# A hybrid S5 and GLA layer on one core: the GLA passes moved ahead of the S5 scan, scan temporaries in PSUM

## The chip, the cores and the metric

The kernel runs on one core of a Trainium2 chip. The metric is the time of one execution in microseconds (us). The five engines of the core work from queues of their own: PE is TensorE (matrix products; PEld are its weight loads), DVE is VectorE, ACT is ScalarE, POOL is GpSimd, and SP only issues DMAs here. They meet through semaphores alone.

## The reference

One layer over 512 latent tokens (`lat`) and 256 context tokens (`ctx`) of width 1024, in fp32: a half-step SwiGLU (ffn1), a token mixer, a second half-step SwiGLU (ffn2), a last norm. Each is preceded by an RMS norm with shift and scale and followed by a gate; these nine vectors come from a linear map of the conditioning (`ada_w`, nine groups of 1024 columns). The mixer, cut to what matters:

```python
u, q, k, v, r, glr, ga, gb = split(h @ w_in)            # 512,256,256,512,512,32,1024,1024
ya = s5_branch(u)      # per group of 16 channels: h_t = lam * h_(t-1) + B u_t (complex, 64 states),
                       # both directions; y = gelu(Re(C h) + d u); ya = y * sigmoid(y @ glu_w + b)
yb = gla_branch(q, k, v, glr)   # chunks of 64 tokens, 4 heads, both directions:
                       # log decay = logsigmoid(glr @ gate_up + b) / 16, cumulated in the chunk,
                       # masked scores q k^T inside, a carried state k^T v across chunks
yb = rms_norm(yb) * silu(r)
y = (sigmoid(ga) * (ya @ s5_out) + sigmoid(gb) * (yb @ gla_out)) @ w_o
```

## The kernel before

**Products.** Each fp32 product is made of three matmuls: every weight block and every moving block is split in a high and a low part, and `split_mm` (L795) adds lo*hi, hi*lo and hi*hi. Weights come in units of 512 KB. SP loads them into four slots of `w_raw`; POOL makes `w_hi` (L724) and `w_lo` (L727) of each, 3.5 us in all, once the last job that used the slot four units before is done (`last_user`). The order of units is written out in the table UNIT.

**Jobs.** TensorE's work is numbered in the table JOB. Job j writes PSUM slot j % 4: `lat(j)` is its even bank, `ctx_(j)` its odd bank (eight banks of 512 fp32). TensorE may start job j when slot_read says that job j - 4 was read; it adds to job_done at its end. A job of a projection with 128 output channels is 24 matmuls of 512 columns (`tall_jobs`, L1013), with 24 more of 256 if the context is wanted (k, v, glr). u is made of 8 jobs (`wide_jobs`, L996), each for every eighth token and with all four slots of weights.

**Order of TensorE in the mixer.** u (8 jobs, the first waits for one row of h after another while `norm` makes them), glr, k, ada7, q, ada8, the chunks (transposes `ut` of u, the four r, `xs`: state inputs of the scan), v (4), its transposes vt (6), ga (8), gb (8), z0 (gate logits), y (8 jobs: S5 outputs from ut, the scanned states xs and hb, with three matrices per group streamed from HBM into `stream2`), yt, z1, glu (4). Then four GLA passes p (two head pairs x two directions): ket (transposes of the decayed keys), sc (scores, two jobs), kv (two jobs), and after every second pass out (4 jobs). Eight products of `ya @ s5_out`, called ma, are spread between them (`MA_AFTER`). Then ybt (transposes of the GLA output), mb (8 products of `yb @ gla_out`), wo (8), the norm and ffn2.

**The S5 scan** runs on DVE alone (`advance`, L1961 on, called 21 times): five tensor_tensor instructions a step, a product with the real part of a power of lambda (L1980), two halves with the imaginary part (L1981, L1982), two additions to `xs` (L1984, L1986). Powers (`lam_p`) and temporaries (`st1`, `st2`) lie in SBUF. Its steps: three over the context (16, 8 and 4 blocks of 64 elements), 7 of 512 elements, 7 of 64, 4 of 896. It begins when ACT has read the last xs job and must end before y (states_ok).

**GLA chain of one pass.** ACT's `softplus(p)` reads z (three activations, table loads between), DVE's `cumulate(p)` makes the cumulated decays (L2027 to L2036), ACT's `decays(p)` the exponentials, DVE's `decayed(p)` the scaled q and k (L2043 to L2052), then ket and sc on TensorE, ACT copies ket, DVE masks the scores (L2095) and after kv carries the states (L2118, L2120; s_ok). Its buffers lie where h was, so nothing of it could start before gb was done.

**ada groups.** DVE adds up each of the late groups from eight tiles of 512 KB in a ring of two (`ada_add`); group 7 and 8 are loaded at the mixer's start, and TensorE sums each in ada_job.

The head of the chunks' order and the place of the products ma:

```python
CHUNK_ORDER = [("ut", 4), ("r", 1), ("ut", 4), ("r", 1), ("xs", 6), ("r", 1), ("xs", 6), ("r", 1), ("xs", 4)]
MA_AFTER = {("kv", 0): 2, ("kv", 1): 2, ("kv", 2): 1, ("kv", 3): 2, ("out", 3): 1}
```

## Time and profile before

| | |
|---|---|
| median of 3 runs | 1567.67 us (1566.15 to 1569.5) |
| profiled execution, its own time | 1567.58 us |
| its span | 1565.6 us |
| mean granted clock of TensorE | 0.966 |
| busy: PE, PEld, DVE, ACT, POOL | 93%, 81%, 48%, 17%, 43% |
| mixer, first matmul of u to first of wo | 683.7 to 1127.5 us |

A busy TensorE may still run at half its clock (1.2 instead of 2.4 GHz); the column PEclk of a stretch gives the mean granted clock, 1.00 being 2.4 GHz. Idle time is told with the engine or DMA whose semaphore ended it.

### The profile page before, as it was taken

How to read it: one execution, taken by the hardware profiler on the slowest of the kernel's cores; microseconds unless marked ns; L12 is line 12 of the kernel's file. 1: busy time of each engine (PE TensorE's matmuls, PEld its weight loads, DVE VectorE, ACT ScalarE, POOL GpSimd, SP SyncE). 2: the span in 40 equal slices, each digit the busy share in tenths (PEclk: the TensorE clock that was granted, in tenths of full speed). 3: DMA queues.
4: the chain of work that ended last, by engine and by line, in shares of the span. 5: the costliest groups of instructions: out<-in, count | busy, mean ns of one | idle time of the engine just before them, and what ended most of it. 6: DMA issues, size and time to landing. Idle time of an engine off the chain costs nothing.

```text
span 1565.6 us, 18786 instructions
## 1 busy us (share of the span) xinstructions
PE 1461.8 (93%) x7780; PEld 1261.9 (81%) x7780; DVE 757.3 (48%) x1004; ACT 268.5 (17%) x418; POOL 675.9 (43%) x389
## 2 busy tenths in 40 slices
...
GB/s 295 93 186 61 111 148 111 105 148 103 123 150 74 132 153 41 56 93 99 174 154 102 122 128 159 156 16 23 139 135 67 82 107 95 94 95 93 105 72 54
DMA packets 232561, 174.28 MB, mean 111 GB/s; under 512 B 28664, under 2 KB 212124, under 8 KB 232476
## 3 DMA queue, kind: packets, MB, share of 16 engines
...
q8 instruction: 61, 1.00, 0.3%
...
HBM read 155.26 MB, written 17.79 MB: 111 GB/s over the span
## 4 chain that ended last, share of the span: by engine, by line
PE 85%; DVE 8%; ACT 2%; issue 2%; SPq 1%; DMA 0%; DVEq 0%; POOL 0%; ACTq 0%; PEldq 0%; POOLq 0%
PE ps L795 58%; PE ps L966 14%; PE ps L969 4%; PE ps L826 2%; PE ps L804 2%; DVE ssq L1763 1%; PE ps L888 1%; PE ps L879 1%; PE ps L1055 1%; DVE h_lo L1799 1%; SPq L663 1%; PE ps L1204 1%; PE ps L1208 1%; DVE gu L1785 0%; DVE y L2068 0%
## 5 line engine op out<-in xcount | busy, mean ns | idle before, releaser
L724 POOL TENSOR_SCALAR w_hi<-w_raw 128x1024 fp32r<-128x1024 f32 (+2 forms) x187 | 214.0, 1145 | 825.2 <-issue 464.2
L727 POOL TENSOR_TENSOR w_lo<-w_raw,w_hi 128x1024 fp32r<-128x1024 f32 (+2 forms) x187 | 460.2, 2461 | 15.6
L795 PE MATMUL ps<-h_hi,w_lo 128*128 128x384 f32 (+2 forms) x1344 | 419.8, 361 | 13.1 <-DVE h_lo L1799 5.6
L795 PE MATMUL ps<-h_lo,w_hi 128*128 128x384 f32 (+2 forms) x1344 | 415.0, 358 | 0.0
L795 PE MATMUL ps<-h_hi,w_hi 128*128 128x384 f32 (+2 forms) x1344 | 414.9, 358 | 0.0
L795 PEld LDWEIGHTS ps<-h_hi,w_lo 128*128 128x128 f32 (+1 forms) x1344 | 241.4, 188 | 45.1 <-issue 7.1
L795 PEld LDWEIGHTS ps<-h_hi,w_hi 128*128 128x128 f32 (+1 forms) x1344 | 244.0, 188 | 24.2
L795 PEld LDWEIGHTS ps<-h_lo,w_hi 128*128 128x128 f32 (+1 forms) x1344 | 244.0, 188 | 23.4
L1840 DVE SCALAR_TENSOR_TENSOR ps<-ps,silu 128x768 f32<-128x768 f32 (+1 forms) x44 | 36.6, 832 | 283.5 <-PE ps L795 283.5
L1864 DVE SCALAR_TENSOR_TENSOR x<-ps,mod,x 128x512 f32<-128x512 f32 x96 | 70.7, 748 | 171.5 <-PE ps L969 94.0
L966 PE MATMUL ps<-act_hi,w_lo 128*128 128x512 f32 x352 | 140.2, 398 | 1.8 <-DVEq L1845 1.8
L966 PE MATMUL ps<-act_lo,w_hi 128*128 128x512 f32 x352 | 138.4, 393 | 0.0
L966 PE MATMUL ps<-act_hi,w_hi 128*128 128x512 f32 x352 | 138.3, 393 | 0.0
L1384 ACT ACTIVATE silu<-ps 128x768 f32<-128x768 f32 (+1 forms) x44 | 31.1, 707 | 514.4 <-PE ps L795 514.3
L1742 DVE SCALAR_TENSOR_TENSOR ada_acc<-ada_w,cs,ada_acc 128x1024 f32<-128x1024 f32 x70 | 100.7, 1471 | 21.7 <-DMA ada_w<-in_ada_w_dram 20.4
L1397 ACT ACTIVATE act_hi<-ps 128x768 fp32r<-128x768 f32 (+1 forms) x44 | 31.1, 707 | 316.0 <-DVE ps L1840 316.0
L966 PEld LDWEIGHTS ps<-act_hi,w_lo 128*128 128x128 f32 x352 | 66.6, 189 | 20.2 <-DVEq L1845 4.7
L966 PEld LDWEIGHTS ps<-act_hi,w_hi 128*128 128x128 f32 x352 | 66.4, 189 | 14.7
L966 PEld LDWEIGHTS ps<-act_lo,w_hi 128*128 128x128 f32 x352 | 66.4, 189 | 14.5
L1843 DVE TENSOR_TENSOR act_lo<-ps,act_hi 128x768 fp32r<-128x768 f32 (+1 forms) x44 | 36.3, 825 | 37.4 <-ACT act_hi L1397 37.4
L969 PE MATMUL ps<-act_hi,w_lo 128*128 128x256 f32 x176 | 49.4, 280 | 0.0
L969 PE MATMUL ps<-act_hi,w_hi 128*128 128x256 f32 x176 | 49.3, 280 | 0.0
...
## 6 DMA issues: line engine op xcount, KB each, us to landing
...
```

The lines of the kernel that those rows point to most:

```text
L724: pool.tensor_scalar(w_hi[:, s, 0:cols], w_raw[:, s, 0:cols], 1.0, 1.0, ALU.mult, ALU.mult)\
L727: pool.tensor_tensor(w_lo[:, s, 0:cols], w_raw[:, s, 0:cols], w_hi[:, s, 0:cols].bitcast(F32), ALU.subtract).then_inc(w_split, 1)
L795: last = pe.matmul(mv[2], st, mv[part], start=(first and q == 0), stop=(n == len(terms) - 1 and q == 2))
L804: return pe.transpose(o, i, ident[0:i.shape[0], 0:i.shape[0]])
L826: last = pe.matmul(o, cs[:, k, :], first_tile(g, k)[:, 512 * q:512 * q + 512], start=(k == 0), stop=(k == KD - 1))
L966: last = pe.matmul(lat(j), st[:, k, c], mv[:, k, 0:NL], start=(k == 0 and r == 0), stop=(k == tiles - 1 and r == 2))
L969: last = pe.matmul(ctx_(j)[:, 0:NC], st[:, k, c], mv[:, k, NL:NT], start=(k == 0 and r == 0), stop=(k == tiles - 1 and r == 2))
L1384: act.activation(dst, src, ACT.Silu).then_inc(slot_read[jg % 4], 1)
L1742: STT(acc, tile, cs[:, k, v:v + 1], acc, ALU.mult, ALU.add).then_inc(acc_ok, 1)
L1840: STT(up, up, 0.5, sl, ALU.mult, ALU.mult).then_inc(gu_ok, 1)
L1843: TT(lo, up, hi.bitcast(F32), ALU.subtract).then_inc(act_lo_ok, 1)
L1864: ins = STT(x[:, k, 0:NL], lat(j), mod[:, g, 0:1], x[:, k, 0:NL], ALU.mult, ALU.add)
```

## The change

The mixer's work is put in another order, and buffers are laid out anew for it; the products and their number stay the same.

- TensorE starts with k0, k1 and q0 together, one k-step of all three for each row of h; then glr, q1, z0, z1, ada7, v and vt. The GLA passes follow (`GLA_ORDER`), with four of the gb products (gbA) and the eight u jobs between their steps in place of ma; then the chunks with ybt among them, gbB (4), ga (8), y, yt, mbA (4), glu (4), mbB (4), ma (8), wo.
- The scan's powers lie in the odd PSUM banks 1 and 3 and its temporaries in banks 5 and 7. A bank holds 512 elements, so the step of 1024 becomes two of 512 and the four of 896 become eight of 448: 26 calls. The powers are made in SBUF (`lam_s`) and copied.
- Scores use 64 of the 128 rows (kz, qz without zero halves), in one job over both banks of a slot.
- The GLA product is kept in SBUF times its gate (`mb`), and the S5 product is made last and added to it. sigmoid and product of the GLU are written back to PSUM.
- SP: the S5 output matrices of the first three batches are loaded earlier, gates later; v3's weights stand between tiles 1 and 2 of ada group 7. Group 8 is loaded in ffn2's first segment, a tile behind each weight unit, added by DVE there, summed by TensorE behind the last up product of that segment.

```diff
+_number(UNIT, [("ffn1", FFN_UNITS), ("k", 2), ("q0", 1), ("glr", 1), ("q1", 1), ("v", 4), ("gbA", 4), ("u", 4), ("r", 4),
+               ("gbB", 4), ("ga", 8), ("mbA", 2), ("glu", 2), ("mbB", 2), ("ma", 4), ("wo", 8), ("ffn2", FFN_UNITS)])
+GLA_ORDER = [("ket", 0, 1), ("sc", 0, 1), ("kv", 0, 2), ("gbA", 0, 1), ("gbA", 1, 1), ("z", 2, 1),
+             ("ket", 1, 1), ("sc", 1, 1), ("kv", 1, 2), ("gbA", 2, 1), ("out", 1, 4), ("gbA", 3, 1), ("z", 3, 1),
+             ("ket", 2, 1), ("sc", 2, 1), ("kv", 2, 2), ("u", 0, 1), ("u", 1, 1), ("u", 2, 1),
+             ("ket", 3, 1), ("sc", 3, 1), ("kv", 3, 2), ("u", 3, 1), ("u", 4, 1), ("u", 5, 1), ("u", 6, 1),
+             ("out", 3, 4), ("u", 7, 1)]
-CHUNK_ORDER = [("ut", 4), ("r", 1), ("ut", 4), ("r", 1), ("xs", 6), ("r", 1), ("xs", 6), ("r", 1), ("xs", 4)]
+CHUNK_ORDER = [("ut", 4), ("r", 1), ("ut", 4), ("r", 1), ("xs", 6), ("r", 1), ("xs", 6), ("r", 1), ("ybt", 4), ("xs", 4)]
...
+    def lam_p(c):
+        return ps[:, 2 * c + 1, :].rearrange("p (k g) -> p k g", g=DG)
+    def scan_part(c, shape):
+        return ps[:, 5 + 2 * c, 0:int(np.prod(shape))].rearrange("p (k g) -> p k g", g=DG)
...
@@ SP
+                        if not with_ada and part.segs + i == 0:
+                            ada_tile(ADA_MIX + 1, v)
...
+            for k in range(KD):
+                ada_tile(ADA_MIX, k)
+                if k == 1:
+                    tall(UNIT["v"] + 3, 1, C_V + 3 * P)
+            tall(UNIT["gbA"], 4, C_GB)
+            wide(UNIT["u"], C_U)
+            tall(UNIT["r"], 4, C_R)
...
+            for b in range(3):
+                y_matrices(b)
+            tall(UNIT["ga"] + 4, 4, C_GA + 4 * P)
+            half_units("mbA", out_b, 0)
+            half_units("glu", glu_w, 0)
+            is_done(sp, JOB["ga"] + 7)
...
+            for t in range(4):
+                load_gate(KD + t)
+            for b in range(3, 8):
+                y_matrices(b)
@@ TensorE
+            first = [("k", 0, JOB["k"], NT), ("k", 1, JOB["k"] + 1, NT), ("q0", 0, JOB["q0"], NL)]
...
+            for k in range(KD):
+                pe.wait_ge(h_ok, KD + k + 1)
+                for i in range(len(first)):
...
+            tall_job("glr", 0, JOB["glr"], NT, 2 * RANK)
+            tall_job("q1", 0, JOB["q1"], NL)
+            gate_logits(0)
+            gate_logits(1)
+            ada_job(ADA_MIX, JOB["ada7"])
+            for q in range(4):
+                tall_job("v", q, JOB["v"] + q, NT)
...
+            for t in range(6):
+                was_read(pe, JOB["vt"] + t)
...
+                for t in range(4):
+                    for hp in range(2):
+                        r = slice(64 * hp, 64 * hp + 64)
+                        last = pe.matmul((lat, ctx_)[hp](j)[:, P * t:P * t + P], kz[r, P * t:P * t + P],
+                                         e1q[r, P * t:P * t + P], start=True, stop=True)
@@ ACT
+            softplus(0)
+            softplus(1)
+            evac_tokens(JOB["v"], v_t[:, 0, :], NT, P)
+            decays(0)
+            for q in range(1, 4):
+                evac_tokens(JOB["v"] + q, v_t[:, q, :], NT, P)
+            decays(1)
+            for t in range(6):
+                take_v(t)
+            take_keys(0)
+            for q in range(2):
+                take_gate(GJ["gbA", q], KD + q)
+            softplus(2)
+            take_keys(1)
+            decays(2)
+            take_gate(GJ["gbA", 2], KD + 2)
+            take_out(1)
+            take_gate(GJ["gbA", 3], KD + 3)
+            softplus(3)
+            take_keys(2)
+            decays(3)
...
@@ DVE
+            for p in range(4):
+                masked(p)
+                states(p)
+                if p < 3:
+                    decayed(p + 1)
+                if p < 2:
+                    cumulate(p + 2)
...
-                TT(t1, prev, c_re, ALU.mult).then_inc(scan_step, 1)
-                TT(part(t2, low), part(prev, high), part(c_im, high), ALU.mult).then_inc(scan_step, 1)
-                TT(part(t2, high), part(prev, low), part(c_im, low), ALU.mult).then_inc(scan_step, 1)
+                TT(part(0, every), prev, c_re, ALU.mult).then_inc(scan_step, 1)
+                TT(part(1, slice(*low)), rows(prev, high), rows(c_im, high), ALU.mult).then_inc(scan_step, 1)
+                TT(part(1, slice(*high)), rows(prev, low), rows(c_im, low), ALU.mult).then_inc(scan_step, 1)
                 dve.wait_ge(scan_step, n0 + 1)
-                TT(cur, cur, t1, ALU.add).then_inc(scan_step, 1)
+                TT(cur, cur, part(0, every), ALU.add).then_inc(scan_step, 1)
                 dve.wait_ge(scan_step, n0 + 4)
-                TT(cur, cur, t2, ALU.add).then_inc(scan_step, 1)
+                TT(cur, cur, part(1, every), ALU.add).then_inc(scan_step, 1)
...
+            def ya_low(c):
+                j = JOB["glu"] + c
+                dve.wait_ge(yah_ok, c + 1)
+                TT(ya_lo[:, c, :], lat(j), ya_hi[:, c, :].bitcast(F32), ALU.subtract).then_inc(slot_read[j % 4], 1)
```

## Rows read from the trace of the kernel before

**Rows 1.** Page part 1: busy time of TensorE, share of the span, instructions.
```profile
PE 1461.8 (93%) x7780; PEld 1261.9 (81%) x7780; DVE 757.3 (48%) x1004; ACT 268.5 (17%) x418; POOL 675.9 (43%) x389
```

**Rows 2.** Page part 4: the chain that ended last, shares of the span by engine.
```profile
PE 85%; DVE 8%; ACT 2%; issue 2%; SPq 1%; DMA 0%; DVEq 0%; POOL 0%; ACTq 0%; PEldq 0%; POOLq 0%
```

**Rows 3.** Five stretches: length; busy us (x instructions) of PE, PEld, DVE, ACT, POOL; clock; DMA share; GB/s.
```profile
683.70:740.90 57.20, 53.15 (x192) 45.84 (x192) 24.01 (x34) 10.89 (x20) 1.99 (x6) 0.84 0.34 111
825.00:950.60 125.60, 123.97 (x600) 103.98 (x600) 120.84 (x120) 19.23 (x32) 73.01 (x37) 1.00 0.40 108
950.60:981.30 30.70, 24.30 (x197) 21.99 (x196) 13.85 (x17) 16.84 (x22) 1.79 (x2) 1.00 0.78 220
981.30:1005.00 23.70, 16.54 (x84) 12.87 (x85) 18.60 (x12) 15.62 (x17) 17.40 (x9) 0.78 0.19 61
1005.00:1095.00 90.00, 70.09 (x577) 56.43 (x575) 61.34 (x95) 30.55 (x49) 14.55 (x8) 0.89 0.17 54
```

**Rows 4.** List of waits of TensorE: who waited for whom, total us, times, longest.
```profile
PE ps L804 <- DVE ke L2047: 8.8, 2, 4.7
PE ps L795 <- DVE y_lo L2063: 6.3, 1, 6.3
PE ps L804 <- DVE o_sb L2135: 5.8, 1, 5.8
PE ps L804 <- ACT v_t L1442: 1.6, 1, 1.6
PE ps L795 <- POOL w_lo L727: 1.4, 1, 1.4
```

**Rows 5.** Timeline of PE, first projection: start, us, instruction, [idle before <- releaser].
```profile
697.36 0.76 PE L795 MATMUL ps<-w_hi,h_lo 128*96 128x512 f32 x1 [0.93 <-DVE h_lo L1799]
...
702.13 0.40 PE L795 MATMUL ps<-w_hi,h_hi 128*96 128x512 f32 x1
702.37 0.40 PE L795 MATMUL ps<-w_hi,h_lo 128*96 128x512 f32 x1
```

**Rows 6.** Timeline of DVE: adds of ada group 7.
```profile
711.14 1.28 DVE L1742 SCALAR_TENSOR_TENSOR ada_acc<-ada_w,cs,ada_acc 128x1024 f32<-128x1024 f32 x1 [2.05 <-DMA ada_w<-in_ada_w_dram]
714.09 1.29 DVE L1742 SCALAR_TENSOR_TENSOR ada_acc<-ada_w,cs,ada_acc 128x1024 f32<-128x1024 f32 x1 [1.66 <-DMA ada_w<-in_ada_w_dram]
```

**Rows 7.** Timelines of DVE and ACT: one softplus, cumulate and decays; take_v.
```profile
861.51 3.05 ACT L1474 ACTIVATE v_sb<-ps 128x512 f32<-128x512 f32 x6 [0.98 <-PE ps L804]
...
957.65 1.02 DVE L2027 TENSOR_SCALAR g_b<-ps,vt 128x768 f32<-128x768 f32 x1 [1.93 <-ACT g_a L1492]
...
963.19 0.63 ACT L1499 ACTIVATE g_a<-g_b 128x512 f32<-128x512 f32 x1 [1.99 <-DVE g_d L2036]
...
965.88 0.69 DVE L2043 TENSOR_TENSOR e1q<-qt,g_a 128x512 f32<-128x512 f32 x1 [2.72 <-ACT g_c L1503]
```

**Rows 8.** Timeline of DVE: the S5 scan and the copy to hb.
```profile
825.44 2.04 DVE L1980 TENSOR_TENSOR st<-xs,lam_p 128x1024 f32<-128x1024 f32 x1 [36.30 <-ACT xs L1467]
...
865.51 0.69 DVE L1980 TENSOR_TENSOR st<-xs,lam_p 128x512 f32<-128x512 f32 x1
...
869.12 0.69 DVE L1980 TENSOR_TENSOR st<-xs,lam_p 128x512 f32<-128x512 f32 x1
...
876.31 2.77 DVE L1980 TENSOR_TENSOR st<-xs,lam_p 128x512 f32<-128x512 f32 x1
...
895.46 0.22 DVE L1980 TENSOR_TENSOR st<-xs,lam_p 128x64 f32<-128x64 f32 x1
...
950.79 1.23 DVE L2013 COPY hb<-xs 128x2048 f32<-128x2048 f32 x1 [0.66 <-PE ps L795]
```

**Rows 9.** Groups of DVE by form: x count | busy, mean ns | idle before.
```profile
L1864 DVE SCALAR_TENSOR_TENSOR x<-ps,mod,x 128x512 f32<-128x512 f32 x96 | 70.7, 748 | 171.5 <-PE ps L969 94.0 <-PE ps L966 77.5
...
L1763 DVE TENSOR_TENSOR ssq<-ssq,silu 128x512 f32<-128x512 f32 x14 | 14.6, 1042 | 0.3
```

More of the change, by code:

```diff
@@ new lines @@
+_number(JOB, [("vec", 1), ("x", KD), ("skip", 2), ("xh", 14), ("row1", 1), ("row0", 1), ("col1", 1), ("col0", 1), ("lam", 1),
+              ("ffn1", FFN1_JOBS), ("norm1", 2), ("k", 2), ("q0", 1), ("glr", 1), ("q1", 1), ("z0", 1), ("z1", 1),
+              ("ada7", 1), ("v", 4), ("vt", 6), ("gla", GLA_JOBS), ("chunks", 32), ("gbB", 4), ("ga", 8), ("y", 8),
+              ("yt", 4), ("mbA", 4), ("glu", 4), ("mbB", 4), ("ma", KD), ("wo", KD), ("norm2", 2), ("ffn2", FFN2_JOBS),
+              ("norm3", 1), ("out", 4)])
@@ L163 @@
 NADA = 9 * KD
 GJ = {("z", 0): JOB["z0"], ("z", 1): JOB["z1"]}
[L169 to L170 removed]
 def _gla_jobs():
     n = JOB["gla"]
[L175 to L183 removed]
+    for name, p, count in GLA_ORDER:
+        GJ[(name, p)] = n
+        n += count
@@ L950, in seg @@
                             last = ada_sums(ada_cols(j, ADA_COL), g)
+                        if not two and nth == 0 and v == 2 * tiles - 1:
+                            pe.wait_ge(acc_ok, ada_added(ADA_MIX + 1, KD))
+                            last = ada_sums(ada_late(j), ADA_MIX + 1)
                         last.then_inc(job_done, 1)
@@ new lines, in _, with gate_logits @@
+            tall_job("glr", 0, JOB["glr"], NT, 2 * RANK)
+            tall_job("q1", 0, JOB["q1"], NL)
+            def gate_logits(p):
+                ti, d = p // 2, p % 2
+                j = GJ["z", p]
+                wait_read(pe, j)
+                for q in range(2):
+                    last = pe.matmul((lat, ctx_)[q](j)[:, 0:384], gate_up[:, d, P * ti:P * ti + P],
+                                     glr[:, 384 * q:384 * q + 384], start=True, stop=True)
+                last.then_inc(job_done, 1)
@@ new lines, in _ @@
+            for name, p, _ in GLA_ORDER:
+                if name == "ket":
+                    turn_keys(p)
+                elif name == "sc":
+                    scores(p)
+                elif name == "kv":
+                    key_values(p)
+                elif name == "out":
+                    readout(p)
+                elif name == "z":
+                    gate_logits(p)
+                elif name == "gbA":
+                    tall_job("gbA", p, GJ["gbA", p], NL)
+                else:
+                    wide_job("u", GJ["u", p], lambda h, k: h[:, k, p:NT:CH], NCH)
@@ L1060, in state_inputs, with turn_o @@
                     pe.sem_inc(st_used, 1)
+            def turn_o(c, j):
+                pe.wait_ge(ybtok_ok, 1)
+                wait_read(pe, j)
+                for t in range(4):
+                    last = transpose(lat(j)[:, P * t:P * t + P], o_sb[:, t, P * c:P * c + P])
+                last.then_inc(job_done, 1)
             for name, b, j in CHUNK_JOBS:
@@ L1215, in _ @@
[L1215 to L1223 removed]
+            for i in range(4):
+                out_product("mbA", i, JOB["mbA"] + i, yb_hi, yb_lo, None if i else yb_ok)
@@ L1224, in _ @@
+            for i in range(4):
+                out_product("glu", i, JOB["glu"] + i, y_hi, y_lo, None if i else yl_ok)
+            for i in range(4):
+                out_product("mbB", i, JOB["mbB"] + i, yb_hi, yb_lo)
+            for c in range(4):
+                was_read(pe, JOB["glu"] + c)
+            for i in range(KD):
+                out_product("ma", i, JOB["ma"] + i, ya_hi, ya_lo)
             for q in range(KD):
@@ L1509, in _ @@
+            for q in range(4):
+                take_gate(JOB["gbB"] + q, KD + 4 + q)
+            for q in range(8):
+                take_gate(JOB["ga"] + q, q)
+            for c in range(4):
+                was_read(act, CJ["ybt", c])
+                act.activation(yb_hi[:, c, :], r_sb[:, c, :], ACT.Copy).then_inc(ybh_ok, 1)
             for b in range(8):
                 j = JOB["y"] + b
-                if b == 2:
-                    decays(0)
                 is_done(act, j)
```

888 lines of the change are left out of this document (411 added, 477 removed).

## The prediction

> **What bounds the kernel now.** I read the page first, then the chain, then stretches, then single waits. TensorE is busy 93% of the span [rows 1], and 85% of the chain that ended last runs over it, with DVE next at 8% [rows 2]. So only two things pay: time in which TensorE stands or runs at the lower clock, and work that leaves it. The change alters no product of the projections, so I look for standing time. The stretches [rows 3] show where it is in the mixer: 4.0 of 57.2 us idle at mean clock 0.84 while u is projected, almost none between 825 and 950.6, then 6.4 of 30.7 at the S5 outputs, 7.2 of 23.7 (clock 0.78) around the GLU product and 19.9 of 90 (clock 0.89) in the GLA passes. In the list of waits [rows 4] the reader should see that nearly all of it is TensorE waiting for a chain of DVE and ACT operations with no product beside it.
>
> The profiled execution took 1567.58 us by its own time, of which the span is 1565.6; the median of the three runs is 1567.67. I sum against 1567.6.
>
> **Part 1, the first projections.** Before, u starts one k-step each time norm() has made an h row: 192 matmuls take 57.2 us [rows 3]. Their full-speed spacing is 0.24 us [rows 5] at 702.13 and 702.37, nearer 0.2365 over the run of them, so 45.4 us is work and 11.7 is waiting and low clock. The clock came back only 4.8 us after the work became dense at 697.36 [rows 5]. After the change each k-step carries k0, k1 and q0: 9 matmuls of 512 and 6 of 256 columns, about 2.8 us at full and 5 at half rate, against a step of the norm of 2.2. TensorE never waits after its first step; I charge only a low-clock start of 4.6 us, half of which is lost. Saved: 11.7 - 2.3 = **9.4**. The 1.4 us for w_lo of glr [rows 4] goes too, because glr's weights are split before the norm ends: **1.4**. Bounds: 6 to 11 together with it.
>
> **Part 2, a new wait at ada7.** ada_job(7) now stands ahead of v, so TensorE meets it early. By work, k, q and glr end about 38.9 us after 683.7, and z0, z1 take 3: 725.6. The adds of group 7 run off a ring of two tiles, one per 2.8 us (711.14 to 714.09 is one step [rows 6]). On SP the weights of v3 now stand between tiles 1 and 2, and wait for the split of q1, which POOL can start only when k0 is done (about 707) and which takes 3.5. So tile 2 is issued near 710.5 instead of 707.3, the two transfers share the queue, and the last add ends near 729.8. Cost: 4.2 of waiting plus a low-clock spell. For a spell I take 2.2 us, from the GLA passes below. **+6.4**, bounds 0 (tiles as punctual as before) to +9. Behind the waiting TensorE stand v and all of the GLA passes. ada8 moves into ffn2: its TensorE time only changes place.
>
> **Part 3, v and its transposes.** The v evacuation waited 1.6 us [rows 4]. Now decays(1) stands between the last v evacuation and take_v on ACT (a decays took 2.7, DVE's wait at 965.88 [rows 7]), and all six take_v must end before ket0, 3 us for six [rows 7]. I count 4.8 of waiting for 1.6: **+3.2**, bounds +1 to +5.
>
> **Part 4, the GLA passes.** Before, from ket0 (1005.0) to the first full-speed mb job (1106.8): 101.8 us. TensorE stands for 19.9 of the 90 us up to 1095 [rows 3] and another 5.8 for o_sb [rows 4], about 26 us. Work at full speed is 64.2: four passes of 4.1, two z of 1.5, out 19.6, ma 21.8, ybt 2, the start of mb 1.4. So 11.6 is low clock. The list of waits has five long ones in it, two of them the 8.8 for ke [rows 4]: 2.3 or so each, and 2.2 is the price I use above. After, gate products gbA and u stand between the steps. What still waits: (a) kv1 and kv2. take_keys(p) stands behind softplus(p) on ACT, and one softplus from the end of z to the first DVE use took 5.5 us (z ended at 952.1, DVE starts at 957.65 [rows 7]); plus the copy of ket 0.95, minus ket and sc 2.6: 3.8 each. (b) out1: softplus 5.4, cumulate 5.5 (957.65 to 963.19 [rows 7]), masked 1.3, states 4.3 make 16.5 after z2, while TensorE has 13.2 to 15 of work with gbA2: 2. (c) passes 0 and 3 have gate or u products enough. Waits 9.4 to 9.6, three spells 6.6: 16 against 37.6. Saved: **21.6**. DVE operations with two SBUF inputs may stretch beside the splits of the gbA and u weights, that is the upper bound; no spells at all is the lower: 14 to 28.
>
> **Part 5, chunks.** ut0 waits for the evacuation of u7 (0.9), and r0 for a split that can begin only when u7 frees its slot: 3.5 less 2 of transposes, 1.5. **+2.4**. ybt is moved in, counted above. bounds +1 to +4.
>
> **Part 6, the scan, the largest term.** Before, advance() ran from 825.4 to 950.1 [rows 8], 124.7 us, and v, vt, ga and gb, 125.6 us [rows 3], covered it to the microsecond. After, only four gb and eight ga products follow the last xs: 12 at 5.45 (24 matmuls of 0.227) = 65.5. So the question is how long the scan takes. The same instruction, 512 elements, took 0.69 at 865.51 and 2.77 at 876.31 [rows 8]; POOL was busy 73 of these 125.6 us [rows 3]. Instructions that read one operand from PSUM don't show this: 96 of x<-ps,mod,x have mean 748 ns, against 1042 for the same 512 elements of ssq<-ssq,silu, both inputs in SBUF [rows 9], though POOL splits weights beside both. In the new advance() each of the five instructions has exactly one PSUM operand (lam_p or scan_part) among its inputs. So I take undisturbed prices: 512 elements 0.72 apart (865.51 to 869.12 is five), 64 elements 0.22 long and 0.26 apart, 448 by interpolation 0.66; plus 0.02 for PSUM. Steps: 10 of 512 x 3.7, one of 256 2.4, 7 of 64 x 1.35, 8 of 448 x 3.4: 76, and the copy of hb 1.3 [rows 8]. TensorE waits 77.3 + 0.5 - 65.5 = 12.3 where it waited for nothing, and y0 and y1 then run at the low clock: 2.6. **+14.9**, bounds +10 (no PSUM surcharge, no spell) to +25 (some PSUM latency on each of 130 instructions).
>
> The Trainium skill, page "SBUF — State Buffer", section "Who interferes with whom", says that a DVE instruction with two SBUF inputs contends with a GpSimd one that reads SBUF, and one with at most one SBUF input doesn't. The rows agree on both halves; by that rule the scan would be the 76 us above.
>
> **Part 7, y, yt and what follows.** The first three y batches are loaded early, but the fourth is issued only when y0 is done, and SP needs 3.7 us a batch, as before: **-0.4**. From yt to the end of glu it was 23.7 us [rows 3] for 13.8 of work: waits 6.3 for y_lo [rows 4], 0.8, and low clock. Now mbA (10.9) lies over the y_lo chain; only its first job waits 2 for a slot. Saved **7.9**, bounds 5 to 9. The new GLU chain through PSUM is covered by mbB, 2.7 a product against some 2.1 on DVE. The last product's tail to wo (gate, add, m_hi, m_lo) is the same with ma as with mb.
>
> **Part 8, ffn2.** SP now stands at ada tile 2 of group 8 until DVE, busy with norm(2), adds tile 0, and the fourth weight unit is queued behind. It would land about 5 us after the norm and be split as TensorE arrives: **+1**, bounds 0 to +6.
>
> **Sum:** -9.4 - 1.4 + 6.4 + 3.2 - 21.6 + 2.4 + 14.9 - 0.4 - 7.9 + 1 = -12.8. 1567.6 - 12.8 is about **1554.8 us**.
>
> **Rivals.**
> A, slower: the scan keeps its stretch under POOL's splits although an operand lies in PSUM, for instance because one SBUF operand is enough to collide. Its undisturbed price before was 68.9 by the same table, it took 124.7, a factor of 1.8; 76 becomes 137, and TensorE waits 61 us more: 1616. It decides early: at a scan of 76 + 12.8 = 89 us the whole gain is gone. Against it speak 96 instructions of one length [rows 9]. 6%.
> B, smaller or no gain: the serial parts (softplus, cumulate, masked, states) stretch beside POOL, the adds of group 7 come late and ffn2 starves. Upper bounds of parts 2, 4 and 8 together: +2.6 + 7.6 + 5 = 15, so 1555 to 1570. 34%, of which 12% is still more than 3 us faster, 14% is no difference and 8% lies beyond it.
> C, more gain: clock spells stay away where waits are near 4 us; five of them at 2.2 and an early ada7: -15 more, 1540. 14%.
> The forecast, 1548 to 1560, has 46%.
>
> **How the numbers follow.** The slower cases are A with 6% and the far end of B with 8%; 0.2%, or 3.1 us, is about what a measurement of this kernel can tell from no change. Faster 0.46 + 0.14 + 0.12 = 0.72, same 0.14, slower 0.14. The range must leave out no more than two in ten: A and the worst of B above, the extreme of C below: 1539 to 1569.
>
> **What would show it.** Right: no wait inside the first three jobs after 683.7; scan instructions of 512 elements all near 0.70 while POOL is busy; one wait of about 12 us before y; no wait between yt and glu. Wrong: scan instructions of 2 us and more (A); waits at ket, kv and out of more than 5 us each (B); a granted clock of 1.00 through the GLA passes (C). Most likely to be wrong is the 12 us before y, as the difference of two long numbers, and how often the clock falls.

## The result, and the profile after

The changed kernel takes 1556.46 us (median of 7 executions, 1552.68 to 1559.47) against 1567.67 (7 executions, 1564.57 to 1573.38): a ratio of 0.9924, 95% interval [0.9905, 0.9943]. That is 11.2 us less, where 12.8 were forecast (1554.8). The profiled execution took 1557.78 us, its span is 1556.0, 9.6 less than the span of before.

Busy time of the page, and the chain that ended last. They answer to [rows 1] and [rows 2]:

```profile
PE 1460.2 (94%) x7780; PEld 1263.5 (81%) x7780; DVE 701.1 (45%) x1021; ACT 272.0 (17%) x421; POOL 665.7 (43%) x389
PE 82%; DVE 10%; ACT 2%; issue 2%; DMA 1%; SPq 1%; POOL 0%; DVEq 0%; ACTq 0%; POOLq 0%; PEldq 0%
```

TensorE is as busy as before to 2 us: what went is time in which it stood. DVE's share of the chain has grown, from 8 to 10%, although its busy time fell by 56 us: the scan is shorter, but it is now seen. The waits of TensorE in the mixer answer to [rows 4] (who waited for whom, total us, times, longest):

```profile
PE ps L1245 <- DVE hb L2213: 10.0, 1, 10.0
PE ps L924 <- DVE ada_acc L1837: 9.2, 1, 9.2
PE ps L1141 <- ACT ket L1537: 8.6, 2, 4.3
PE ps L840 <- ACT v_sb L1531: 2.5, 2, 1.6
PE ps L1158 <- DVEq L2102: 1.7, 1, 1.7
PE ps L840 <- ACT v_t L1497: 1.6, 1, 1.6
PE ps L831 <- POOL w_lo L763: 1.5, 1, 1.5
```

The 8.8 for ke, 6.3 for y_lo and 5.8 for o_sb are gone. In their place stand the end of the scan (hb) and the sums of ada7. The copy of ket is not new: the kernel before waited for it once, for longer, in a line that [rows 4] do not show:

```profile
PE ps L1187 <- ACT ket L1546: 5.1, 1, 5.1
```

By stretches (columns as in [rows 3]), in the order of the parts: first projections, z and ada7's wait, v and vt, GLA passes with gbA and u, chunks, the products over the scan, the wait, y, yt with mbA, GLU to ma:

```profile
684.80:709.80 25.00, 24.96 (x120) 21.28 (x121) 16.30 (x28) 8.25 (x15) 3.36 (x7) 0.89 0.36 128
709.80:723.70 13.90, 13.90 (x73) 9.51 (x71) 4.28 (x2) 3.69 (x5) 13.57 (x8) 1.00 0.47 151
723.70:735.80 12.10, 2.88 (x9) 1.40 (x9) 7.76 (x5) 11.46 (x11) 5.58 (x3) 0.68 0.68 190
735.80:784.10 48.30, 42.96 (x232) 37.51 (x233) 17.58 (x19) 14.82 (x26) 14.51 (x8) 0.90 0.26 72
784.10:902.10 118.00, 107.70 (x768) 93.34 (x768) 46.72 (x81) 33.78 (x51) 14.44 (x8) 0.97 0.15 41
902.10:950.90 48.80, 44.02 (x274) 38.39 (x273) 22.57 (x23) 17.60 (x48) 22.10 (x14) 0.97 0.41 109
950.90:1016.40 65.50, 65.50 (x288) 53.94 (x288) 61.65 (x132) 8.13 (x14) 43.60 (x25) 1.00 0.58 169
1016.40:1026.50 10.10, 0.09 (x2) 0.05 (x1) 9.74 (x16) 4.07 (x6) 3.40 (x2) 0.75 0.41 130
1026.50:1056.70 30.20, 25.31 (x192) 23.67 (x193) 2.30 (x4) 4.73 (x8) 0.00 (x0) 0.91 0.63 182
1056.70:1074.20 17.50, 15.66 (x81) 13.01 (x82) 6.51 (x7) 8.96 (x9) 3.44 (x2) 0.80 0.30 98
1074.20:1117.70 43.50, 43.50 (x194) 36.03 (x193) 22.04 (x33) 8.71 (x15) 27.59 (x16) 1.00 0.62 194
```

From the mixer's first matmul to the first of wo it is 432.8 us (684.84 to 1117.67) against 443.7, from there to the end 438.3 against 438.2, and the mixer starts 1.1 us later.

The scan by form (count, busy us, mean ns), in the 65.5 us of which POOL was busy for 43.6:

```profile
L2180 DVE TENSOR_TENSOR ps<-xs,ps 64x512 f32<-64x512 f32 x10 | 7.0, 698 | 0.3
L2179 DVE TENSOR_TENSOR ps<-xs,ps 128x512 f32<-128x512 f32 x10 | 7.0, 695 | 3.5 <-ACT xs L1622 3.2
L2185 DVE TENSOR_TENSOR xs<-xs,ps 128x512 f32<-128x512 f32 x10 | 6.9, 686 | 0.3
```

Every instruction of 512 elements takes 0.67 to 0.70 us: the forecast's sign of part 6. The scan ran from 951.3 to 1025.1. The first instruction of all its steps, and two that follow each other in the first step:

```profile
L2179 DVE TENSOR_TENSOR ps<-xs,ps x29: 228/629/697, 951.3 to 1022.0; 128x512 f32<-128x512 f32 x10, 128x64 f32<-128x64 f32 x10, 128x448 f32<-128x448 f32 x8, 128x256 f32<-128x256 f32 x1
952.75 0.69 DVE L2181 TENSOR_TENSOR ps<-xs,ps 64x512 f32<-64x512 f32 x1
953.36 0.67 DVE L2183 TENSOR_TENSOR xs<-xs,ps 128x512 f32<-128x512 f32 x1
```

It has 29 steps, ten of them of 64 elements, not 26 with seven; the kernel before has 24, not 21 (its L1980 stands 24 times in the trace, ten times with 64 elements).

### The profile page after: what moved, and what is told of

Same layout as the page of the kernel before. It is cut to its first block, busy times and chain, and to the rows that moved or that the text cites. A ratio compares the mean times of both kernels' runs of the same rounds, so it can differ in the third digit from the quotient of the medians.

```text
span 1556.0 us, 18816 instructions
## 1 busy us (share of the span) xinstructions
PE 1460.2 (94%) x7780; PEld 1263.5 (81%) x7780; DVE 701.1 (45%) x1021; ACT 272.0 (17%) x421; POOL 665.7 (43%) x389
## 4 chain that ended last, share of the span: by engine, by line
PE 82%; DVE 10%; ACT 2%; issue 2%; DMA 1%; SPq 1%; POOL 0%; DVEq 0%; ACTq 0%; POOLq 0%; PEldq 0%
PE ps L831 53%; PE ps L1005 14%; PE ps L1008 4%; PE ps L862 2%; PE ps L840 2%; PE ps L1077 2%; PE ps L924 1%; DVE ssq L1858 1%; PE ps L915 1%; PE ps L1206 1%; DVE xs L2185 1%; DVE ps L2180 1%; DVE ps L2181 1%; DVE ps L2179 1%; DMA ada_w<-in_ada_w_dram 1%
## 5 line engine op out<-in xcount | busy, mean ns | idle before, releaser
L760 POOL TENSOR_SCALAR w_hi<-w_raw 128x1024 fp32r<-128x1024 f32 (+1 forms) x187 | 211.4, 1131 | 824.5 <-issue 438.0
L763 POOL TENSOR_TENSOR w_lo<-w_raw,w_hi 128x1024 fp32r<-128x1024 f32 (+1 forms) x187 | 452.8, 2421 | 15.6
L831 PE MATMUL ps<-h_hi,w_lo 128*128 128x384 f32 (+3 forms) x1304 | 411.4, 364 | 12.5 <-DVE h_lo L2006 4.8
L831 PE MATMUL ps<-h_lo,w_hi 128*128 128x384 f32 (+3 forms) x1304 | 405.6, 360 | 0.0
L831 PE MATMUL ps<-h_hi,w_hi 128*128 128x384 f32 (+3 forms) x1304 | 405.1, 359 | 0.0
L831 PEld LDWEIGHTS ps<-h_hi,w_lo 128*128 128x128 f32 (+1 forms) x1304 | 237.1, 189 | 44.3 <-issue 12.4
L831 PEld LDWEIGHTS ps<-h_hi,w_hi 128*128 128x128 f32 (+1 forms) x1304 | 239.2, 189 | 23.2
L831 PEld LDWEIGHTS ps<-h_lo,w_hi 128*128 128x128 f32 (+1 forms) x1304 | 239.5, 189 | 22.4
L1837 DVE SCALAR_TENSOR_TENSOR ada_acc<-ada_w,cs,ada_acc 128x1024 f32<-128x1024 f32 x70 | 105.2, 1535 | 24.2 <-DMA ada_w<-in_ada_w_dram 22.3
L1005 PEld LDWEIGHTS ps<-act_hi,w_hi 128*128 128x128 f32 x352 | 66.4, 189 | 15.5
L1008 PE MATMUL ps<-act_lo,w_hi 128*128 128x256 f32 x176 | 49.7, 283 | 0.0
```

Of the source, the lines that this page charges most:

```text
L760: pool.tensor_scalar(w_hi[:, s, 0:cols], w_raw[:, s, 0:cols], 1.0, 1.0, ALU.mult, ALU.mult)\
L763: pool.tensor_tensor(w_lo[:, s, 0:cols], w_raw[:, s, 0:cols], w_hi[:, s, 0:cols].bitcast(F32), ALU.subtract).then_inc(w_split, 1)
L831: last = pe.matmul(mv[2], st, mv[part], start=(first and q == 0), stop=(n == len(terms) - 1 and q == 2))
L1005: last = pe.matmul(lat(j), st[:, k, c], mv[:, k, 0:NL], start=(k == 0 and r == 0), stop=(k == tiles - 1 and r == 2))
L1008: last = pe.matmul(ctx_(j)[:, 0:NC], st[:, k, c], mv[:, k, NL:NT], start=(k == 0 and r == 0), stop=(k == tiles - 1 and r == 2))
L1837: STT(acc, tile, cs[:, k, v:v + 1], acc, ALU.mult, ALU.add).then_inc(acc_ok, 1)
```

## The experiments

Twelve kernels, each with runs of the kernel before beside it. Ratios are to those runs. A difference "to the changed kernel" is the ratio less 0.9924, times 1568 us; with both intervals it is good to about 4 us, so where less matters the traces are compared as well. All diffs are against the changed kernel.

**1. Is it PSUM that keeps the scan short?**

```diff
 def lam_p(c):
-    return ps[:, 2 * c + 1, :].rearrange("p (k g) -> p k g", g=DG)
+    return lam_t[:, SUP * c:SUP * c + SUP, :]
 def scan_part(c, shape):
-    return ps[:, 5 + 2 * c, 0:int(np.prod(shape))].rearrange("p (k g) -> p k g", g=DG)
+    return scan_tmp[:, c, 0:int(np.prod(shape))].rearrange("p (k g) -> p k g", g=DG)   # SBUF, at u_at
```

> The changed kernel with one thing undone: the scan's powers and its two temporaries lie in SBUF again (in the place of lam_t and in that of u_tok), every instruction of the scan is otherwise the same, and so is every other engine's work. My theory (part 6): an operand in PSUM is what keeps the scan clear of POOL's splits. Then the 512-element instructions take 2 us and more while POOL is busy. In the kernel before, 68.9 us of undisturbed work took 124.7 with POOL busy for 73 of them, so 1 us of busy POOL costs the scan about 0.76 us. POOL has some 50 us of splits beside the scan here, so the scan takes about 69 + 38 = 107 instead of 73.8 us, the wait before y grows from 10 to about 43, and the time is about 1590 us (1580 to 1600). Rival 1: PSUM has nothing to do with it and the scan is fast because POOL's splits fall otherwise: the scan takes 69 to 74 us, the time is 1551 to 1557. Rival 2: one PSUM input is enough for half of it: 1565 to 1575.

Measured: 1596.32 us (1594.29 to 1597.5), ratio 1.0173 [1.0156, 1.019], 39 us more than the changed kernel and slower than the kernel before. DVE's timeline at the start and at the end of the scan, and the two stretches of the scan:

```profile
949.53 2.32 DVE L2180 TENSOR_TENSOR scan_tmp<-xs,lam_t 128x512 f32<-128x512 f32 x1 [3.19 <-ACT xs L1623]
951.88 1.41 DVE L2181 TENSOR_TENSOR scan_tmp<-xs,lam_t 64x512 f32<-64x512 f32 x1
953.33 2.77 DVE L2182 TENSOR_TENSOR scan_tmp<-xs,lam_t 64x512 f32<-64x512 f32 x1
...
960.39 0.69 DVE L2180 TENSOR_TENSOR scan_tmp<-xs,lam_t 128x512 f32<-128x512 f32 x1
...
1022.41 0.69 DVE L2180 TENSOR_TENSOR scan_tmp<-xs,lam_t 128x512 f32<-128x512 f32 x1
...
1026.03 0.23 DVE L2180 TENSOR_TENSOR scan_tmp<-xs,lam_t 128x64 f32<-128x64 f32 x1
...
1065.02 1.23 DVE L2214 COPY hb<-xs 128x2048 f32<-128x2048 f32 x1
```
```profile
950.90:1016.40 65.50, 63.77 (x282) 52.47 (x280) 64.07 (x45) 7.88 (x14) 50.04 (x27) 1.00 0.56 164
1016.40:1068.00 51.60, 1.70 (x8) 1.70 (x9) 48.32 (x106) 2.78 (x4) 2.55 (x1) 0.51 0.07 23
```

The same instruction takes 0.69, 1.41 or 2.77 us (the first 2.32) while POOL splits weights. While TensorE's products last, DVE gets 45 instructions done instead of 132; only when POOL has no more to split does it run at its own pace, and TensorE waits 51.6 us for hb instead of 10.0. The theory holds. 107 us of scan were expected, and it took 115.5 (949.53 to 1065.02). The stretch itself came out as expected, 38 us: at the undisturbed prices of this trace's end (a step of 512 elements 3.62 us, of 64 1.28, of 448 3.28, and 2.3 for the one of 256) the 29 steps take 77.5. What was wrong is the base of 69, the price of the kernel before's fewer and larger steps with three of 64 elements left out. Rivals 1 and 2 fall.

**2. Why did ada7 wait 9.2 us?** The adds of DVE in the changed kernel; they answer to [rows 6]:

```profile
707.93 1.29 DVE L1837 SCALAR_TENSOR_TENSOR ada_acc<-ada_w,cs,ada_acc 128x1024 f32<-128x1024 f32 x1 [0.67 <-DMA ada_w<-in_ada_w_dram]
718.32 4.38 DVE L1837 SCALAR_TENSOR_TENSOR ada_acc<-ada_w,cs,ada_acc 128x1024 f32<-128x1024 f32 x2 [9.11 <-DMA ada_w<-in_ada_w_dram]
724.30 1.73 DVE L1837 SCALAR_TENSOR_TENSOR ada_acc<-ada_w,cs,ada_acc 128x1024 f32<-128x1024 f32 x1 [1.59 <-DMA ada_w<-in_ada_w_dram]
727.03 4.80 DVE L1837 SCALAR_TENSOR_TENSOR ada_acc<-ada_w,cs,ada_acc 128x1024 f32<-128x1024 f32 x2 [1.00 <-DMA ada_w<-in_ada_w_dram]
734.46 1.28 DVE L1837 SCALAR_TENSOR_TENSOR ada_acc<-ada_w,cs,ada_acc 128x1024 f32<-128x1024 f32 x1 [2.63 <-DMA ada_w<-in_ada_w_dram]
```

Tile 2 is added at 718.32, 7.2 us later than in the kernel before, and pairs of adds beside POOL take 4.4 and 4.8 us instead of 2.6.

```diff
 for k in range(KD):
     ada_tile(ADA_MIX, k)
-    if k == 1:
-        tall(UNIT["v"] + 3, 1, C_V + 3 * P)
+tall(UNIT["v"] + 3, 1, C_V + 3 * P)
```

> The changed kernel with one issue moved on SP: the weights of v3 are requested behind all eight tiles of ada group 7 instead of between tiles 1 and 2. My theory (part 2, the term that I mis-sized): v3's place, behind the split of q1, is what delays tile 2 from 711 to 718 us. Then tile 2 is issued as DVE adds tile 0, the last add ends near 728 instead of 735.7, TensorE waits about 2 us instead of 9.2 at ada7, and less work runs at the low clock: 7 to 9 us less, about 1548.5 us (1547 to 1550). Rival 1: the adds are slow because POOL's splits stretch them (two of them took 4.4 and 4.8 us for two), not because of the order: wait at ada7 stays at 6 us or more, 1553 to 1556. Rival 2: v3 comes late instead and its own job waits: 1552 to 1558.

Measured: 1548.82 us (1548.42 to 1555.3), ratio 0.9882 [0.9857, 0.9906], 6.6 us less than the changed kernel. Tile 2 is added at 712.14, the last at 726.65, and TensorE waits 0.55 us for ada_acc. So most of the wait was the place of one weight unit on SP. How much varies between executions: with the same place the three kernels of experiment 8 waited 2.4, 3.0 and 2.5 us in their traces, and the first kernel of experiment 6, with the old place, 6.9. v3's own job did not wait more than before (rival 2). Two adds still took 4.75 us beside POOL (rival 1), but a stream that starts in time absorbs it.

**3. The waits for ket, and where saved waiting went.**

```diff
-("gbA", 0, 1), ("gbA", 1, 1), ("z", 2, 1), ... ("out", 1, 4), ("gbA", 3, 1), ("z", 3, 1),
+("gbA", 0, 1), ("z", 2, 1), ("gbA", 1, 1), ... ("out", 1, 4), ("z", 3, 1), ("gbA", 3, 1),
```

> The changed kernel with two jobs exchanged twice in the GLA passes: the gate logits z2 stand ahead of gate product gbA1 (and z3 ahead of gbA3), with ACT's order to match, so that softplus(p) has 5.5 us of product over it. My theory (part 4): the two waits of 4.3 us for ket are the softplus that stands ahead of take_keys on ACT. Then both waits fall below 0.5 us, and the two low-clock spells beside them (1.7 us lost in each) go: 8 to 12 us less, about 1546 us (1544 to 1549). Rival 1: another chain on DVE (masked, states, decayed) is next to come late and takes most of it back as waits at out1 or ket2: 1551 to 1555. Rival 2: TensorE's saved time is lost again later, because the weight splits or the outer loads set the pace: 1555 to 1557.

Measured: 1556.08 us (1547.4 to 1558.84), ratio 0.9904 [0.9867, 0.9942]: 3 us less, within what can be told. Three of the four executions took 1555.4 to 1558.8, at mean granted clocks of 0.964 to 0.966, the fourth 1547.4 at 0.970; the trace is of one of the three. The edit did what it says: the two waits for ket, 8.6 us, became 1.5. One wait grew, from 1.7 us, that of the read-out of pass 1 (list of waits of this kernel):

```profile
PE ps L1158 <- DVEq L2102: 2.8, 1, 2.8
```

What the read-out behind it took is the answer. First the changed kernel's stretch, then this kernel's read-out and what follows:

```profile
816.70:826.60 9.90, 9.84 (x96) 7.52 (x96) 4.55 (x4) 1.15 (x3) 2.04 (x1) 1.00 0.28 78
```
```profile
812.06:829.70 17.64, 17.64 (x96) 13.21 (x96) 3.39 (x4) 1.15 (x3) 0.80 (x1) 0.50 0.16 43
829.70:840.40 10.70, 10.70 (x36) 7.44 (x34) 2.03 (x3) 7.41 (x8) 0.37 (x1) 0.71 0.00 0
```

The same 96 matmuls took 9.9 us at clock 1.00 and 17.6 at 0.50 (1.2 GHz). TensorE came to them out of a wait, and the level did not come back while the small matmuls ran, only in the projection that followed. In this execution saved waiting was given back as low clock. Neither rival as written (a chain on DVE, an outer load) is what the trace shows.

**4. The price of the wait before y.**

```diff
-for h in range(LCH // SUP):
+for h in range(3):
```

> The changed kernel with part of the computation left out: of the last stage of the scan (8 steps of 448 elements, 3.4 us each) only 3 are made, so the scan ends some 17 us earlier and its states are incomplete. It prices the wait before y with its low clock. My theory: TensorE loses the wait of 10.0 us there and 1.7 to 2.6 us in the low-clock spell that follows: about 1544.3 us (1543.5 to 1545). Rival 1: the spell costs nothing, 1546.5. Rival 2: something else is late at that point (the first y matrices, the gate products on their way out) and keeps TensorE waiting: 1548 or more.

Measured: 1542.49 us (1539.97 to 1543.28), ratio 0.9829 [0.9812, 0.9845], 15 us less. In its trace no wait stands before y. From the end of the last state input to the first of yt it is 93.8 us instead of 105.8, and the first four mbA take 12.8 instead of 13.6: 12.9 us in all, a wait of 10.0 and 2.9 of low clock, most of it in y0. The spans of the two traces differ by 15.5; the other 2.6 are no part of the price, since they lie ahead of the scan, where the two kernels do the same (the last state input ends 2.9 us earlier here). Rival 1 (the spell is free) falls, and nothing else was late (rival 2).

**5. The read-out without a wait ahead of it.**

```diff
-("kv", 1, 2), ("gbA", 2, 1), ("out", 1, 4), ("gbA", 3, 1), ("z", 3, 1), ("ket", 2, 1), ...
+("kv", 1, 2), ("gbA", 2, 1), ("gbA", 3, 1), ("out", 1, 4), ("z", 3, 1), ("u", 0, 1), ("ket", 2, 1), ...
```

> The changed kernel with another order in the GLA passes: z2 ahead of gbA1 as in e3_z_ahead, and both gbA2 and gbA3 stand between kv1 and the read-out of pass 1; z3 follows the read-out and u0 stands between z3 and ket2. In e3_z_ahead the two waits for ket (8.6 us) went to 1.5 us and yet three of four runs were no faster: the trace has the clock low from the wait of 2.8 us ahead of out1 through the whole read-out, which took 18.8 us instead of 9.8. My new theory: what was saved as waiting is given back as low clock in the read-out, because TensorE comes to it out of a wait. With no wait ahead of it the read-out runs at full clock: 8 to 12 us less than the changed kernel, about 1546.5 us (1544 to 1549). Rival: the read-out's small matmuls lower the clock by themselves whenever fewer projections stand around them: the read-out takes 18 us again, 1553 to 1557.

Measured: 1543.77 us (1541.35 to 1547.91), ratio 0.9847 [0.9822, 0.9873], 12 us less. The read-out is back at 9.9 us, and the rival (small matmuls lower the clock by themselves) falls. In experiment 3 they ran at the low clock after a wait of 2.8 us; here, with no wait ahead, at 1.00.

**6. GLU ahead of mbA, and the old y_lo chain.** The first of three kernels puts mbA behind GLU again:

> The changed kernel with one thing undone: the GLU product stands directly behind the transposes yt again, and the four mbA products behind it. My theory (part 7): mbA covers the chain y_hi, y_lo on ACT and DVE. Without it TensorE waits about 6.3 us for y_lo, as before, and runs some more work at the low clock: 7.9 us more, about 1564.3 us (1561.5 to 1565.5). Rival 1: the low-clock spell of 6.8 us at yt is there in both, so only the waits differ, 6.3 less the 1.8 that mbA waits for: +4.5, about 1561 us. Rival 2: the cover is given back behind it (the gated product's chain through PSUM, the outer loads), 1555 to 1558.

Measured: 1556.59 us (1555.19 to 1560.59), ratio 0.9926 [0.9907, 0.9946], the same as the changed kernel. TensorE's timeline at yt:

```profile
1051.95 2.20 PE L840 MATMUL ps<-ident,y_tok 64*128 64x64 f32 x32 [0.88 <-ACT y_tok L1634]
1055.97 0.76 PE L831 MATMUL ps<-y_hi,w_lo 128*128 128x512 f32 x1 [1.82 <-DVEq L2227]
1056.54 0.63 PE L831 MATMUL ps<-y_lo,w_hi 128*128 128x512 f32 x1
...
1059.59 0.80 PE L831 MATMUL ps<-y_hi,w_lo 128*128 128x512 f32 x1 [0.22 <-DVE y_lo L2224]
```

GLU begins 1.8 us after yt, as mbA does in the changed kernel, but runs longer at the low clock. I had read the 6.3 us of [rows 4] as the length of a chain that needs cover. Before, GLU waited for the fourth y_lo; the change lets it go on with each as it comes. The second kernel puts that back, in this order:

```diff
-TT(y_lo[:, c, :]..., lat(j)..., y_hi..., ALU.subtract)              # each k-step waits for its own
+TT(y_lo[:, c, :], y32[:, c, :], y_hi[:, c, :]..., ALU.subtract)     # y32 is made ahead of y_hi
+pe.wait_ge(yl_ok, 4)                                                # ahead of GLU
```

> e6_mb_behind_glu came out at 1556.6 us, no different from the changed kernel: without mbA over it TensorE waits only 1.8 us after yt, not 6.3. So my step (mbA covers the y_lo chain) is wrong, and the gain must come from the chain itself. In the kernel before, GLU waits for all four y_lo, and each takes two operands from SBUF (8.31 us for four, 2.08 each); in the changed kernel each k-step waits for its own y_lo, which reads one operand from PSUM (1.07 to 1.11 us). New theory: this run is e6_mb_behind_glu with the old chain: y_lo from y32 in SBUF, and GLU waits for all four. The fourth y_lo comes 10.5 us after ACT's first copy instead of 8.7, and nothing of GLU runs beside it: GLU starts at 1063 instead of 1056 and ends some 4 us later: 1560.5 us (1559 to 1563). Rival (it is not this chain but softplus(1) and cumulate(1), which stood around it before): no difference from 1556.6.

Measured: 1561.66 us (1559.68 to 1565.74), ratio 0.9948 [0.9935, 0.9961], 3.4 us over experiment 6's first kernel by the ratios. Its timeline at GLU:

```profile
1065.56 0.80 PE L831 MATMUL ps<-y_hi,w_lo 128*128 128x512 f32 x1 [6.86 <-DVE y_lo L2226]
```

The four y_lo took 0.69 us each here although both inputs lie in SBUF, and POOL splits nothing at that point: in this kernel it is the wait for all four that costs, not where the operand lies. In the kernel before POOL did split there, and the same four took longer:

```profile
984.26 8.31 DVE L2063 TENSOR_TENSOR y_lo<-y,y_hi 128x512 fp32r<-128x512 f32 x4 [1.46 <-ACT y_hi L1527]
```

From the first's start to the fourth's end it is 8.3 us there against 6.2 here (1059.29 to 1065.50), and from yt to GLU 11.3 against 9.1.

The third has the old chain, but mbA ahead of GLU as in the changed kernel:

> The changed kernel (mbA ahead of GLU) with the old chain of e9_old_chain_glu_first: y_lo from y32 in SBUF, GLU waits for all four. Theory: mbA's 11 us cover the chain whichever it is, the fourth y_lo is there when GLU starts: 1556.5 us, no difference from the changed kernel (1555 to 1558). Together with e6 and e9 this says whether the shorter chain and the cover are two ways to the same 4 us, of which either is enough. Rival (mbA covers less than its length, because its first job waits and runs at the low clock): 1558 to 1560.

Measured: 1557.67 us (1555.87 to 1560.08), ratio 0.9918 [0.9904, 0.9932], the same as the changed kernel. From yt to the end of the first 48 matmuls behind it the traces have 21.9 us (old chain, GLU first), 19.9 (new chain, GLU first), 17.4 (changed kernel) and 17.2 (old chain, mbA first). Letting GLU go on with each y_lo and the cover each take a part of the same few microseconds, and with the cover the chain no longer matters.

**7. The gate products' cover.** All four gbA stand ahead of ket0, and none between the steps:

> The changed kernel with the cover of part 4 taken away, not the work: all four gate products gbA stand ahead of ket0, none between the steps of passes 0 and 1, z2 and z3 where they were. It prices the cover. Theory: TensorE waits about 7.5 us for ke at ket1 (masked 1.3, states 4.3, decayed 3.5 against z2's 1.5), about 7.5 at the read-out of pass 1 (cumulate 5.5, masked 1.3, states 4.3 against 3.5 of ket, sc, kv), 4.3 at kv2 as now; the waits of 4.3 at kv1, 1.7 at the read-out and 1.6 at ket0 go. That is +11.7 of waiting, and with low clock in the read-out (9 us, as in e3_z_ahead) and in the steps about +18: 1574 us (1568 to 1580). Rival: the waits grow but the clock stays up, 1566 to 1569.

Measured: 1571.27 us (1569.21 to 1575.64), ratio 1.0011 [1.0, 1.0022], 13.6 us more, at which the whole gain of the change is gone. The waits are 4.8 for ke and 6.5 for the read-out (7.5 each expected), and the clock does the rest. ket0 to kv1, the read-out, z3 to kv2:

```profile
804.70:826.50 21.80, 10.31 (x145) 8.05 (x143) 17.98 (x35) 11.49 (x16) 3.41 (x2) 0.75 0.21 59
826.50:844.10 17.60, 17.60 (x96) 13.22 (x96) 2.77 (x4) 1.15 (x3) 0.00 (x0) 0.50 0.00 0
844.10:854.70 10.60, 9.15 (x76) 6.52 (x74) 3.17 (x3) 6.38 (x8) 0.00 (x0) 0.50 0.01 2
```

Only about 3 us of the 13.6 are more waiting (14.5 in all against 11.9), since the two waits for ket fell from 4.3 each to 0.2 and 1.5; the 1.6 ahead of ket0 did not go, it now stands ahead of the first gate product. The rest is clock. The added waiting was over-rated (11.7), the low clock under-rated (6 against some 11).

**8. Better than both.** All three kernels here have the edit of experiment 2. The first has the order of experiment 5 beside it:

> Both changes of order at once: v3's weights behind the ada tiles (e2_v3_behind_ada: 1548.8, 7.6 us less than the changed kernel) and the GLA order of e5_readout_later. They lie 60 us apart and share no wait, so the sums add: 1548.8 - 10 = about 1539 us (1536 to 1542). Rival: TensorE arrives at the GLA passes 10 us earlier than the DVE chain of pass 0 allows, and part of it returns as waits there: 1542 to 1548.

Measured: 1536.87 us (1536.03 to 1537.82), ratio 0.9797 [0.9782, 0.9812]. The two gains (6.6 and 12.1) add to 18.7, measured 19.9. Then one gate product moved from the GLA passes over the scan, and then a second (diff of both against the order of experiment 5):

```diff
-GLA_ORDER: ("gbA", 2, 1), ("gbA", 3, 1), ("out", 1, 4), ("z", 3, 1), ("u", 0, 1), ("ket", 2, 1), ...
+GLA_ORDER: ("u", 0, 1), ("u", 1, 1), ("out", 1, 4), ("z", 3, 1), ("u", 2, 1), ("ket", 2, 1), ...
-("gbA", 4) ... ("gbB", 4)
+("gbA", 2) ... ("gbB", 6)
```

> As e7_v3_and_order, and one gate product (5.5 us) is taken out of the GLA passes and put behind the last state input, where it covers the scan: 13 products instead of 12 stand there; u0 takes its place ahead of the read-out of pass 1. My theory: cover is a stock, the scan takes 74 us whatever stands over it, so the wait before y falls from 10.0 to 4.6 us, and the GLA passes have enough with u0 and u1: 5.5 us less than e7_v3_and_order, about 1533.5 us (1531 to 1537). Rival 1: the GLA passes then have a wait and a low-clock spell of that size: same as e7_v3_and_order. Rival 2: the clock: a wait of 4.6 us before y brings no spell, and another 2 us go: 1531.

> e8_gate_to_scan (1533.5 us) with one more gate product moved from the GLA passes to the scan: 14 products stand over the scan (76 us against 74), u0 and u1 ahead of the read-out of pass 1. Theory: the wait of 4.8 us before y goes and its low clock with it, 5 to 6 us less; passes 2 and 3, with two u products each, still have enough: 1528 us (1526 to 1530.5). Rival: three u products are no longer left for pass 2, ket3 or the last read-out waits and a low-clock spell takes it back: 1532 to 1536.

Measured: 1533.52 us (1530.17 to 1535.96), ratio 0.9774 [0.9753, 0.9795], with one; 1524.2 us (1522.7 to 1525.9), ratio 0.9708 [0.9695, 0.9722], with two. The kernel with one moved product waits 4.8 us before y as expected, but from y0 to yt it takes 31.2 us; the one with two waits for nothing and takes 28.0. Of these 3.2 us 2.5 lie in y0, which still starts at the low clock. So the last 4.8 us of a wait cost 8, in two traces. By the ratios the second product brought 10 us where 5 to 6 were expected, the first 3.6 where 5.5 were. Beside the 8, the traces show 4.3 us in the stretch from ket0 to the end of the products over the scan (223.1 against 218.8), which with one moved product still has low-clock spells. Why they went with the second product was not tried. GLA passes and chunks, the products over the scan, y in the second kernel:

```profile
777.60:920.10 142.50, 136.16 (x992) 119.84 (x992) 69.55 (x103) 49.21 (x96) 30.69 (x18) 1.00 0.23 60
920.10:996.40 76.30, 76.26 (x336) 62.99 (x336) 71.68 (x146) 9.23 (x16) 50.05 (x29) 1.00 0.57 165
996.40:1030.00 33.60, 26.58 (x229) 24.66 (x229) 6.27 (x6) 13.60 (x20) 3.41 (x2) 0.98 0.84 250
```

A clock of 1.00 over 219 us, the same products as the kernel before, 2.9% less time, some 45 us.

## Why the prediction was right, and where it was not

The time came out within 1.7 us of the forecast, but by errors that offset each other. By parts, in us, the measured value from the trace of after against that of before:

| part | forecast | measured | from |
|---|---|---|---|
| 1 first projections, glr | -10.8 | -10.8 | no wait in the first three jobs, all of part 1 over after 38.9 us, as forecast |
| 2 ada7 | +6.4 | +13 | wait 9.2, the sums 3.4 instead of 1.9, v's four jobs 2.4 over 34.1 at the low clock |
| 3 v, vt | +3.2 | +3.8 | waits 1.6, 0.9, 1.6, 1.3 against 1.6 |
| 4 GLA passes | -21.6 | -25.8 | 118.0 less gbA 21.8 and u 45.4 is 50.8; before 101.8 less 25.2 of ma and ybt and mb is 76.6 |
| 5 chunks | +2.4 | +4 | 0.9 and 1.5 as forecast, and a low-clock spell |
| 6, 7 scan, y | +14.5 | +11.1 | wait 10.0, y 30.3 against 29.2 |
| 7 yt, GLU | -7.9 | -6.3 | 17.4 against 23.7 |
| 8 ffn2 | +1 | +0.2 | wo to the end 438.3 against 438.2 |

The measured column sums to -10.8. z0 and z1 take 2.8 us now, of which before only z0's 1.6 lay outside these stretches: +1.3, so -9.5. The two stretches of the mixer and behind it differ by -10.9 and +0.2, so 1.2 us are not accounted for. The spans differ by 9.6, since the mixer starts 1.1 us later.

Of the signs, the first three jobs without a wait, the scan instructions near 0.70 and the one wait before y were there. Between yt and glu TensorE waited once, 1.8 us ahead of mbA, for which part 7 had 2. Of the signs of being wrong none was: the waits for ket stayed under 5 us, and the clock in the GLA passes was 0.97, not 1.00.

- **Part 1, right** in time and in mechanism.
- **Part 2, the size was off by a factor of two.** The step "tile 2 is issued near 710.5" failed. I had v3's unit ready when k0 was done, at 707, plus 3.5 for the split; in the trace q1's split begins at 708.4 and ends at 712.6, SP issues v3's weights at 712.7 and tile 2 at 713.1, and it is added at 718.3, 5.2 us after its issue. The adds that POOL stretched were not in the sum either. Experiment 2 shows that the unit's place makes most of the wait.
- **Part 4, right in direction, with two errors.** The waits for ket were forecast at 3.8 and measured 4.31 and 4.32, by the chain named. But only two short low-clock spells came instead of three longer ones, and the scores were shorter than I charged. Before and after:

```profile
1005.68 1.95 PE L1173 MATMUL ps<-e1q,kz 128*128 128x128 f32 x16
```
```profile
800.83 1.16 PE L1125 MATMUL ps<-e1q,kz 64*128 64x128 f32 x16
```

Sixteen matmuls of 64 rows, alternately in the upper and the lower half of the array, take 1.16 us where sixteen of 128 rows took 1.95. That is 0.8 us in each of four passes that I had not costed, although the diff shows it. The Trainium skill, page "TensorE: Matmul & The Clock Gate", section "Part 3: Packing small matmuls — row/col tiling", says that matmuls in different row groups of the array run concurrently; the two rows agree with it.
- **Part 6, right in the mechanism, near in the number by luck.** 76 us of scan were forecast and 73.8 measured, 65.5 of products and 65.5 measured, 12.3 of waiting and 10.0 measured. But the count of steps was three short: with ten of 64 elements the forecast's own prices give 80. And the prices were too high: the surcharge of 0.02 us for PSUM was not there (0.695 against 0.69), 2.9 us over 145 instructions, and the fourth instruction of a step began 0.61 us after the third and not 0.72 (952.75 to 953.36), some 3 us over 29 steps. Rival A was a real danger, but its factor of 1.8 was too high: with ten steps of 64 it is 1.7 in the kernel before (124.7 over some 73), and in experiment 1, with all operands in SBUF, 1.5 (115.5 over 77.5). That cost 39 us, not 61. The Trainium skill, page "SBUF — State Buffer", section "Who interferes with whom", says that a DVE instruction with two SBUF inputs contends with a GpSimd instruction that reads SBUF, and one with at most one doesn't; the changed kernel and experiment 1 agree with it (0.67 to 0.70 us against up to 2.77).
- **Part 7, right size, wrong reason.** Cover by mbA is worth about 2.5 us with the new chain (19.9 against 17.4 us in the traces; too little to see in the times), all of it in the clock and in two waits of 0.2, since the first wait is 1.8 with either order. Of the other 3.8, 2.0 are GLU's wait, which no longer asks for all four y_lo (21.9 against 19.9). The diff had it, and I read the wait of before as if its release were unchanged. The remaining 1.8 between 23.7 and 21.9 go with the four y_lo, which took 2.1 us longer in the kernel before, beside POOL's splits; the work of z1 lay inside that wait.
- **Part 8, right:** no starvation in ffn2.
- **The clock** was where the forecast was weakest: I priced a spell at 2.2 us wherever it fell, and one of them in a read-out costs 7.7 (17.6 against 9.9). Rival C's edge (1540) needed them gone; experiment 5 comes near it (1543.8) by taking the wait in front of small matmuls away, and with experiment 2's edit beside it the kernels of experiment 8 pass it.
